# Cross attention of a two-block transformer kernel, issued head by head between the weight units

## What is computed

```python
def memory_cross_attention(h, m, wq, wk, wv, wo):
    q = (h @ wq).reshape(b, s, X_HEADS, X_HEAD_DIM)
    k = (m @ wk).reshape(b, nm, X_HEADS, X_HEAD_DIM)
    v = (m @ wv).reshape(b, nm, X_HEADS, X_HEAD_DIM)
    scores = jnp.einsum('bshe,bmhe->bhsm', q.astype(F32), k.astype(F32)) * (X_HEAD_DIM ** -0.5)
    p = jax.nn.softmax(scores, axis=-1)
    o = jnp.einsum('bhsm,bmhe->bshe', p.astype(v.dtype), v)
    return o.reshape(b, s, D_MODEL) @ wo
```

## Time and profile before

| what | value |
|---|---|
| median of the runs | 1284.28 us |
| the profiled execution, its own time | 1293.12 us |
| its span in the profile | 1291.3 us |
| its mean granted TensorE clock | 0.966 of full speed |
| TensorE matmul, weight load | 94%, 81% of the span |
| VectorE, ScalarE, GpSimd | 61%, 46%, 6% |
| DMA | 160 GB/s in the mean |

### The profile page before, as it was taken

One profiled execution on the slowest core, in us unless ns is written; L12 is line 12 of the kernel. 1 busy time (PEld: TensorE's weight loads), 2 busy tenths in 40 slices (PEclk: granted clock), 3 DMA queues, 4 the chain that ended last, 5 costly groups with the idle time before them and its releaser, 6 DMA issues.

```text
span 1291.3 us, 17676 instructions
## 1 busy us (share of the span) xinstructions
PE 1217.2 (94%) x7057; PEld 1049.6 (81%) x7057; DVE 790.2 (61%) x849; ACT 596.3 (46%) x732; POOL 72.5 (6%) x118
## 2 busy tenths in 40 slices
PE   6967899999999999999999999999979988999997
PEld 5855788888899988888888888887769877888886
DVE  6875666666654446666667666666574544666665
ACT  5444653443465655443445434445454544443443
POOL 2010100000002210000000000000011101000000
PEclk8886999999999999999999999999988999999999
DMA  8242445665543446555665556554422543456661
GB/s 211 67 105 96 136 149 193 195 191 183 179 163 131 131 131 196 194 180 182 193 195 161 180 182 193 194 185 153 152 99 98 164 130 113 148 182 193 195 191 69
DMA packets 157222, 206.04 MB, mean 160 GB/s; under 512 B 8936, under 2 KB 130352, under 8 KB 157168
## 3 DMA queue, kind: packets, MB, share of 16 engines
q1 hardware_dynamic: 157168, 205.28, 50.0%
HBM read 203.04 MB, written 1.05 MB: 158 GB/s over the span
## 4 chain that ended last, share of the span: by engine, by line
PE 84%; DVE 7%; ACT 5%; POOL 2%; issue 2%; DMA 1%; SPq 0%; POOLq 0%; ACTq 0%; DVEq 0%
PE outp L722 26%; PE acc L663 18%; PE outp L663 17%; PE outp L724 13%; DVE w_lo L1820 2%; ACT w_hi L1383 2%; PE acc L769 2%; PE outp L692 2%; PE outp L680 1%; DMA raw<-in_even_w_in_dram 1%; DVE arena L1965 1%; ACT xn L1392 1%; POOL arena L1316 1%; PE acc L1243 1%; PE acc L1263 1%
## 5 line engine op out<-in xcount | busy, mean ns | idle before, releaser
L1383 ACT ACTIVATE w_hi<-raw 128x2048 fp32r<-128x2048 f32 x183 | 351.1, 1919 | 466.2 <-PE outp L724 301.4
L1820 DVE TENSOR_TENSOR w_lo<-raw,w_hi 128x2048 fp32r<-128x2048 f32 x183 | 419.2, 2291 | 233.0 <-ACT w_hi L1383 233.0
L722 PE MATMUL outp<-h_pair,w_hi 128*128 128x512 f32 x1408 | 503.0, 401 | 3.3 <-DVE h_pair L1857 3.3
L724 PE MATMUL outp<-h_pair,w_lo 128*128 128x256 f32 x1408 | 397.0, 282 | 0.0
L722 PEld LDWEIGHTS outp<-h_pair,w_hi 128*128 128x128 f32 x1408 | 266.6, 189 | 70.4 <-DVE w_lo L1820 2.3
L724 PEld LDWEIGHTS outp<-h_pair,w_lo 128*128 128x128 f32 x1408 | 268.0, 190 | 1.4
L663 PE MATMUL outp<-w_hi,h_pair 128*128 128x512 f32 (+1 forms) x544 | 156.7, 374 | 2.6 <-DVE w_lo L1820 1.5
L663 PE MATMUL acc<-w_hi,f_hi 128*128 128x512 f32 x352 | 138.2, 393 | 0.0
L663 PE MATMUL acc<-w_lo,f_hi 128*128 128x512 f32 x352 | 137.6, 391 | 0.0
L663 PE MATMUL acc<-w_hi,f_lo 128*128 128x512 f32 x352 | 137.2, 390 | 0.0
L663 PEld LDWEIGHTS outp<-w_hi,h_pair 128*128 128x128 f32 x544 | 99.0, 193 | 21.5 <-DVE w_lo L1820 3.6
(11 more groups left out here) (278 smaller groups left out, 1189.4 us busy)
## 6 DMA issues: line engine op xcount, KB each, us to landing
raw<-in_ffn_w_gate_dram SPq DMA_DIRECT2D x44, 1024.0 KB, 5.6
raw<-in_ffn_w_up_dram SPq DMA_DIRECT2D x44, 1024.0 KB, 5.6
raw<-in_ffn_w_down_dram SPq DMA_DIRECT2D x44, 1024.0 KB, 4.9
raw<-in_odd_w_in_dram SPq DMA_DIRECT2D x12, 1024.0 KB, 5.2
raw<-in_w_in_dram SPq DMA_DIRECT2D x10, 1024.0 KB, 5.3
raw<-in_even_w_in_dram SPq DMA_DIRECT2D x5, 1024.0 KB, 9.2
raw<-in_even_w_out_dram SPq DMA_DIRECT2D x4, 1024.0 KB, 7.5
raw<-in_cross_wk_dram SPq DMA_DIRECT2D x4, 1024.0 KB, 5.8
```

What stands on the lines that cost most here:

```text
L722: nc.tensor.matmul(bank.rearrange("p (a l) -> p a l", l=L), wh, h_pair[:, :, c, :], start=c == 0, stop=c == C - 1, skip_group_check=True)
L724: ins = nc.tensor.matmul(bank[:, 0:L], wl, h_hi[:, c, :], start=False, stop=c == C - 1, skip_group_check=True)
L1383: A(w_hi[:, u % 2, :], raw[:, u % RAW, :], ACT.Copy).then_inc(w_hi_ready, 1)
L1820: tt(w_lo[:, u % 2, :], raw[:, u % RAW, :], w_hi[:, u % 2, :].bitcast(F32), ALU.subtract).then_inc(w_lo_ready, 1)
```

## The change

TensorE, ScalarE and VectorE get a new order in the cross stage. The bank of a score holds one head with both halves of the tokens, and so do the probabilities. The uses of the banks are numbered in the new order. The scores of head 0 come after q1, those of head 1 after q2, those of head 2 after q3; the probabilities of head 0 stand ahead of q3; the first output unit stands between the probabilities of head 2 and those of head 3. The values are split into `m_hi` and `m_lo` in place of `h_hi` and `h_lo`, which the later query units still read. SyncE's list and GpSimd's stay. The number and the sizes of the instructions stay too.

```diff
-                ("norm7", 4), ("xsc", 4), ("xpt", 4), ("xpv", 4),
+                ("norm7", 4), ("xsc0", 1), ("xsc1", 1), ("xpt0", 1), ("xsc2", 1), ("xpt1", 1), ("xpv0", 1),
+                ("xsc3", 1), ("xpv1", 1), ("xpt2", 1), ("xpt3", 1), ("xpv2", 1), ("xpv3", 1),
...
-        xs_tiles = [xs[:, t, 2 * j:2 * j + 2, :] for t in range(T) for j in range(2)]
+        xs_tiles = [xs[:, :, h, :] for h in range(4)]
...
+                def scores_x(h):
+                    k = ACC[f"xsc{h}"]
+                    if h == 0:
+                        out_emptied(pe, OUT["mem_v3"])
+                    out_emptied(pe, OUT["cross"] + h)
+                    acc_taken(pe, k)
...
+                def probs_x(h):
+                    k = ACC[f"xpt{h}"]
+                    acc_taken(pe, k)
+                    pe.wait_ge(p_ready, 6 + h + 1)
+                    for kt in range(T):
+                        for t in range(T):
+                            ins = flip(acc[:, k % NB, kt * L + t * P:kt * L + (t + 1) * P],
+                                       xs[:, t, h, kt * P:(kt + 1) * P])
+                    ins.then_inc(acc_ready, 1)
+
+                def values_x(h):
+                    k = ACC[f"xpv{h}"]
+                    emptied(pe, ACC[f"xpt{h}"])
                     acc_taken(pe, k)
...
+                def out_x(j):
+                    proj_quarter(u0 + 4 + j, OUT["cross_out"] + 2 * (j % 2), j // 2,
+                                 (lambda q: emptied(pe, ACC[f"xpv{q}"])) if j % 2 == 0 else None, (m_hi, m_lo),
+                                 last=j == 3)
+                proj_t(u0, OUT["cross"], fresh=chunks(7))
+                proj_t(u0 + 1, OUT["cross"] + 1)
+                scores_x(0)
+                proj_t(u0 + 2, OUT["cross"] + 2)
+                scores_x(1)
+                probs_x(0)
+                proj_t(u0 + 3, OUT["cross"] + 3)
+                scores_x(2)
+                probs_x(1)
+                values_x(0)
+                scores_x(3)
+                values_x(1)
+                probs_x(2)
+                out_x(0)
+                probs_x(3)
+                values_x(2)
+                values_x(3)
+                for j in range(1, 4):
+                    out_x(j)
...
+                queries(0)
+                split(u0 + 2)
+                queries(1)
+                split(u0 + 3)
+                exps_x(0)
+                queries(2)
+                split(u0 + 4)
+                probs_x(0)
+                exps_x(1)
+                queries(3)
+                split(u0 + 5)
+                exps_x(2)
+                probs_x(1)
+                values_x(0)
+                exps_x(3)
+                values_x(1)
+                probs_x(2)
+                probs_x(3)
+                split(u0 + 6)
+                values_x(2)
+                values_x(3)
+                split(u0 + 7)
+                split(u0 + 8)
...
+                split(u0 + 2)
+                front(0)
+                split(u0 + 3)
+                back(0)
+                front(1)
+                split(u0 + 4)
+                back(1)
+                front(2)
+                split(u0 + 5)
+                back(2)
+                low(0)
+                front(3)
+                low(1)
+                back(3)
+                split(u0 + 6)
+                low(2)
+                low(3)
+                split(u0 + 7)
+                add_last("cross", u0 + 4, OUT["cross_out"])
```

More of the change, by code:

```diff
@@ L1231, in cross @@
                 mem_half("mem_v3", 1)
[L1232 to L1256, removed]
@@ L1257, in cross @@
-                emptied(pe, ACC["xpt"], 4)
-                for h in range(4):
-                    k = ACC["xpv"] + h
+                def scores_x(h):
[5 more added lines that the diff above has]
+                    for t in range(T):
+                        for c in range(2):
+                            ins = nc.tensor.matmul(acc[:, k % NB, t * L:(t + 1) * L],
+                                                   xq_t[:, 2 * h + c, t * P:(t + 1) * P], km_t[:, 2 * h + c, :],
+                                                   start=c == 0, stop=c == 1)
+                    ins.then_inc(acc_ready, 1)
@@ L1266, in cross @@
                     ins.then_inc(acc_ready, 1)
-                proj_out(u0 + 4, OUT["cross_out"], lambda q: emptied(pe, ACC["xpv"] + q))
+                def out_x(j):
[21 more added lines that the diff above has]
+                    out_x(j)
             if "even" in running:
@@ L1645, in acc_copy, with mix_part @@
                 A(dst, src, ACT.Copy).then_inc(acc_free[k % NB], 1)
-            def mix_part(k, c):
+            def mix_part(k, c, hi=h_hi):
                 written(act, k)
-                A(flat(h_hi[:, c:c + 2, :]), acc[:, k % NB, :], ACT.Copy).then_inc(mix_hi, 1)
+                A(flat(hi[:, c:c + 2, :]), acc[:, k % NB, :], ACT.Copy).then_inc(mix_hi, 1)
             def odd():
@@ L1771, in cross, with queries @@
                 mem_copy("mem_v3")
-                for j in range(4):
+                def queries(j):
                     act.wait_ge(w_used, u0 + j + 1)
@@ L1775, in cross, with exps_x, probs_x, values_x @@
                     A(flat(xq_t[:, 2 * j:2 * j + 2, :]), outp[:, k % NB, :], ACT.Copy).then_inc(out_free[k % NB], 1)
[L1776 to L1785, removed]
+                def exps_x(h):
+                    exps(h, 12, xs_tiles[h], 1 / 16, k=ACC[f"xsc{h}"])
+                def probs_x(h):
+                    acc_copy(ACC[f"xpt{h}"], xpt[:, :, h, :], inner=L)
+                def values_x(h):
+                    mix_part(ACC[f"xpv{h}"], 2 * h, m_hi)
+                queries(0)
[21 more added lines that the diff above has]
+                split(u0 + 8)
             if "even" in running:
@@ L1985, in soft_back, with mix_low @@
                 tt(s, s, sm.unsqueeze(2).to_broadcast([P, h, w]), ALU.mult).then_inc(p_ready, 1)
-            def mix_low(n, k, c):
+            def mix_low(n, k, c, hi=h_hi, lo=h_lo):
                 dve.wait_ge(mix_hi, n + 1)
-                tt(flat(h_lo[:, c:c + 2, :]), acc[:, k % NB, :], flat(h_hi[:, c:c + 2, :]).bitcast(F32),
+                tt(flat(lo[:, c:c + 2, :]), acc[:, k % NB, :], flat(hi[:, c:c + 2, :]).bitcast(F32),
                    ALU.subtract).then_inc(acc_free[k % NB], 1)
@@ L2313, in cross, with front, back, low @@
                 split(u0 + 1)
[L2314 to L2323, removed]
+                def front(h):
+                    soft_front(h, 12, xs_tiles[h], 1 / 16, ACC[f"xsc{h}"])
+                def back(h):
+                    emptied(dve, ACC[f"xsc{h}"])
+                    soft_back(h, 12, xs_tiles[h])
+                def low(h):
+                    mix_low(10 + h, ACC[f"xpv{h}"], 2 * h, m_hi, m_lo)
+                split(u0 + 2)
[17 more added lines that the diff above has]
+                add_last("cross", u0 + 4, OUT["cross_out"])
             if "even" in running:
```

## The result

The changed kernel runs in 1281.58 us (median of 20 executions, 1277.29 to 1286.47), the kernel before in 1288.17 (20 executions, 1283.47 to 1293.22). The ratio is 0.9949, with a 95% interval from 0.9934 to 0.9963: faster by 0.51%, 6.6 us. The forecast was a gain of 6.5 us and a time of 1277.8 between 1275.0 and 1280.6. One execution of the kernel before, beside the later experiments, took 4434 us and enters no figure here.

What follows compares the result with a forecast made beforehand. TensorE, busy 94% of the span, bounds the kernel and loses time in the cross stage's attention. Gain 7.1 - 0.3 (borders) - 0.3 (stall) = 6.5 us; median 1284.28 - 6.5 = 1277.8 us, range 1275.0 to 1280.6.

Steps and rivals of the forecast that it cites:

- The pieces of the attention: Cross stage: scores and values 14.0 us plus 16 transposes 2.0 at full clock, 16.0 us in all.
- The borders: TensorE's changes between projections and float32 attention matmuls: three more trips at 0.1 us, 0.3 us lost, bounds zero to 2.5.
- The stall at the seventh matmul of o0: First output unit: its seventh matmul waits about 0.3 us for VectorE's low part of head 1.
- Gross: Cross stage between query and output units: 23.14 us shrinks to 16.0, a gain of 7.1 us before losses.
- norm 9: Feed-forward layer behind the stage starts at half clock, losing 2.4 us; change expected 0, bounds -2.4 to +1.
- A: Tail of the cross stage stays exposed, waits of 1 to 2.5 us; gain 4 to 5.5 us; chance 0.18.
- B: Clock falls inside the new cross stage; gain only 1.7 to 2.7 us; chance 0.09 together with D.
- The rule of the Trainium skill: Against the change: short idle times between PSUM groups can drop the clock; needs one or two us, walk finds 0.3.
- C: Slower: a wait at the first transposes holds the last query unit and all behind it; 1290 us; chance 0.04.
- D: Waits put the sweeps back in order, 5.4 us of idle stay; 1284 us; chance 0.09 together with B.
- E: No borders, no stall, no clock fall behind norm 9; gain 9.5 us, 1274.8 us; chance 0.11.

Runs made afterwards that it cites:

- e5: Changed kernel with the high part of head 1 ahead of the exponentials of head 3 in ScalarE's list; stage 61.38 us, single execution 1278.21 us.
- e4: Changed kernel with the values split into `h_hi` and `h_lo` again, not `m_hi` and `m_lo`; stage 61.31 us, single execution 1273.87 us.
- e2: Kernel before with 34 idle products in TensorE's five longest waits of the mixing layer; 1281.55 us, ratio 0.9949.
- e9: Kernel before with 34 idle products in the mixing layer and 4 ahead of the even layer's 64 small transposes; 1282.43 us, ratio 0.9948.
- e6: Changed kernel's head-by-head order, but with all attention pieces behind the last query unit; stage 66.54 us, 1283.59 us, ratio to the kernel before 0.9964.

## Why the prediction was right in the gain and wrong in the time

**What bounds the kernel, and where it loses.** Right. The walk with durations of before gave the gain of the stage to 0.1 us: 6.5 forecast, 6.56 measured. That it came so close is partly luck, as the terms show.

**The terms of the sum.** Four were off, and they cancelled. The pieces of the attention cost 15.6 us and not 16.0: 1.73 us for a head's scores or values (1049.32 - 1047.59), eight times, and 0.44 for four transposes, four times. The borders cost nothing: the first scores start 0.13 us behind the last matmul of q1 (1029.92 to 1030.05), and the way back shows no more (1030.05 to 1032.00 is 1.95, the 1.73 of the scores and two steps of 0.12). The stall at the seventh matmul of o0 was found at its place, with its cause, and cost 0.44 (e5) in place of 0.3. Not in the sum at all was the new buffer, 0.51 us (e4): the diff names `m_hi` and `m_lo`, and the prediction only asked whether they were free. It is a row that no view of before could give for this unit, but TensorE reads `m_pair` in the memory units too, and I did not look there. Gross 7.5 in place of 7.1 and no borders make 0.7 us more, the larger stall and the buffer 0.65 less: 23.14 - 15.6 - 0.44 - 0.51 = 6.6.

**The step that failed** is the last one of the sum, from the profiled execution to the median: "The profiled execution is 8.8 us above the median of the runs; nothing in the gaps scales with that, so the median goes to 1284.28 - 6.5 = 1277.8." The amount taken away was right and the level that it was taken from was not. The three executions shown, 1283.47, 1284.28 and 1289.91, had two of the lowest group, those under 1286; in the 47 others that group has 13. The median of twenty is 1288.17, and 1288.17 - 6.5 = 1281.7, against 1281.58. The prediction saw a profiled execution 8.8 us above the median and one of three 5.6 us above it. It passed over the first, gave the second a remark in the chances, and made a range of 5.6 us around a level that was uncertain by more. The profiled execution missed in the same way, forecast at 1286.6 and measured at 1282.98: the gain between the two profiles is 10.1, of which 2.7 lie in the mixing layer (137.0 and 134.3 in the table), which the change does not touch. It even had the cause in hand, for norm 9: "Where in them the clock falls may differ from one execution to another; the term is 0, with bounds from -2.4 (no fall) to +1." The same holds at every place where the clock falls, in the mixing layer and at 45 us as well, and the spread of 5.0 and 3.1 us in e2 and e9 (eight and seven executions), against some 10 without idle products, says that these make most of it. A range by the lowest and the highest of the four executions shown, the profiled one with them, would have gone from 1283.5 - 6.5 to 1293.1 - 6.5, that is 1277 to 1286.6, and every measured execution of the change lies in it.

**The rivals.** A, a tail that stays exposed by 1 to 2.5 us, did not come; e6 shows what it looks like when it does. B, a fall of the clock inside the new stage, did not come in the change and came in e6, after a wait of 2.38 us. The rule of the Trainium skill on short idle times between groups ("TensorE: Matmul & The Clock Gate", the second failure mode) was held against this change. What it names, frequent idle times, did not arise: one of 0.18 us is recorded in the stage, and the clock stayed at 1.00. So the run does not speak against the rule. C and D did not come; no wait stands ahead of q3. E had the borders right, at nothing, and the rest wrong: there was a stall, and the clock fell behind norm 9 in the profile after as before.

**The chances.** Faster by over 0.5% had 0.51, and 0.51% was measured (0.37 to 0.66), on the edge where the forecast had put it; on which side it fell is luck.

## What to carry to other kernels

A walk through the lists of the engines with durations from the trace prices a reordering to some tenths of a microsecond, where every piece is known; the points without slack are few, and each can be repaired by name. The level of one launch is another matter: before subtracting a gain from it, look how far the executions lie apart and which stretches of the trace differ in their clock, and make the range at least that wide. A wait of TensorE can cost twice, once as idle time and once as a lower clock behind it (3.48 and 1.2 us in this stage), and where nothing useful can stand in it, idle products can.

## What was new about the hardware

- The same block of 64 small transposes, behind the same wait of 1.10 us, took 9.00 us in four traces of this study and 5.79 in six others without idle products ahead of it, as the clock fell inside it or not. A kernel of 1290 us spreads over 10 us in large part by such places. The Trainium skill ("TensorE: Matmul & The Clock Gate", Part 1) says that the number of matmuls at the lower clock, before the engine reaches the higher one, differs between runs of one kernel. What differs here is whether the clock falls at one place; the start of the kernel was not compared.
- 34 products that compute nothing made this kernel faster by 0.51% (ratio 0.9929 to 0.9969), by holding the clock in one layer of 137 us (e2).
- A wait of 2.38 us was followed by 3.4 us at half clock (e6); the one in the changed kernel, recorded as 0.18 us, was not.
- Going from projections to plain float32 matmuls and back cost nothing that start-to-start times show.
- The stationary operand read from `m_pair` in place of `h_pair` makes an output matmul 0.233 us in place of 0.227 (e4).
